# Latent projections in three mended products, retention's sums inside the next head, the last blocks turned one by one, and one head's value weights loaded aside

## What is computed

```python
# layer 1 of the first block, multi-head latent attention: h is normed and modulated, 768 x 1024
cq   = rms_norm(h @ w_dq, g_q)                  # 1024 -> 384
ckv  = h @ w_dkv                                # 1024 -> 256 + 64
c_kv = rms_norm(ckv[..., :256], g_kv); k_rope = rope(ckv[..., 256:])
# layer 2 of the first block, gated linear attention, 4 heads
q, k, v, gates = h @ w_q, h @ w_k, h @ w_v, log_sigmoid((h @ w1) @ w2 + b)
# layer 2 of the second block, retention, 4 heads of key width 256, value width 512
o = intra + inter                               # 512 tokens x 512 for each head
o = _standardize(o, 1e-6) * silu(gate)          # mean and variance over the 512 values
y = o @ w_out
# the end: layer_norm over 1024, result 512 x 1024
```

## Time and profile before

| | |
|---|---|
| median of 3 runs | 3577.15 us |
| profiled execution: its time, its span | 3580.42 us, 3578.7 us |
| PE busy | 3407.8 us (95%) |
| DVE, ACT, POOL busy | 1955.7, 1265.0, 229.4 us |
| chain that ended last: PE, DVE, ACT, issue, DMA | 86%, 7%, 2%, 2%, 2% |
| mean granted TensorE clock | 0.980 |

### The profile page before, as it was taken

How to read it: one execution, slowest core, us unless ns; L and a number is a source line. 1 busy time by engine, 2 the same in 40 slices (tenths; PEclk the granted TensorE clock), 3 DMA queues, 4 the chain that set the end, 5 groups by cost and what they waited for, 6 DMA issues and landing times.

```text
span 3578.7 us, 46166 instructions
## 1 busy us (share of the span) xinstructions
PE 3407.8 (95%) x17566; PEld 2887.0 (81%) x17566; DVE 1955.7 (55%) x2769; ACT 1265.0 (35%) x1635; POOL 229.4 (6%) x388
## 2 busy tenths in 40 slices
PE   8999989999998999999989999899998999999998
PEld 3799979999987887788868888678787777778886
DVE  4765564445446564645567677577635333454434
ACT  3354552312324333433353344332323222433332
POOL 1110011101000000111100000121100000000000
PEclk9999999999999999999999999999999999999999
DMA  6222123323320111454421111155533222222232
GB/s 231 82 72 65 59 76 111 109 92 118 98 78 30 53 48 59 162 164 156 152 80 36 35 35 48 48 188 188 165 93 101 71 70 70 69 74 94 93 95 80
DMA packets 295528, 335.36 MB, mean 94 GB/s; under 512 B 16497, under 2 KB 264177, under 8 KB 295281
## 3 DMA queue, kind: packets, MB, share of 16 engines
q1 hardware_dynamic: 262352, 232.93, 20.6%
q0 software_dynamic: 29440, 96.49, 8.6%
q10 hardware_dynamic: 3617, 4.26, 0.4%
HBM read 331.55 MB, written 2.10 MB: 93 GB/s over the span
## 4 chain that ended last, share of the span: by engine, by line
PE 86%; DVE 7%; ACT 2%; issue 2%; DMA 2%; DVEq 0%; ACTq 0%; SPq 0%; POOLq 0%; POOL 0%
PE acc L798 67%; PE sc L798 6%; PE sc L1451 2%; PE sc L945 1%; PE acc L1451 1%; PE acc L1644 1%; DVE d_col L2543 1%; PE acc L1060 1%; DMA wring<-in_mlp_w 1%; DVE w_lo L2478 1%; DMA wring<-in_ada_w 1%; PE acc L1423 1%; ACT arena L1847 0%; DVE xT L3042 0%; PE acc L1308 0%
## 5 line engine op out<-in xcount | busy, mean ns | idle before, releaser
L798 PE MATMUL acc<-x_lo,w_hi 128*128 128x512 f32 (+1 forms) x2192 | 826.4, 377 | 1.7 <-DVE xT L3007 1.1
L2478 DVE TENSOR_TENSOR w_lo<-wring,w_hi 128x1024 fp32r<-128x1024 f32 (+3 forms) x444 | 486.6, 1134 | 547.4 <-ACT w_hi L1789 546.5
L1789 ACT ACTIVATE w_hi<-wring 128x1024 fp32r<-128x1024 f32 (+3 forms) x446 | 418.0, 983 | 978.8 <-DMA wring<-in_mlp_w 480.9
L798 PEld LDWEIGHTS acc<-x_lo,w_hi 128*128 128x128 f32 x2192 | 415.2, 189 | 66.7 <-issue 3.1
L798 PE MATMUL acc<-hid_hi,w_hi 128*128 128x512 f32 (+1 forms) x1120 | 412.2, 368 | 5.9 <-DVE arena L2624 3.5
L798 PE MATMUL acc<-hid_hi,w_lo 128*128 128x512 f32 (+1 forms) x1120 | 408.5, 365 | 0.0
L798 PE MATMUL acc<-x_hi_holes,w_hi 128*128 128x512 f32 x768 | 307.9, 401 | 16.4 <-DVE x_lo L2594 13.9
L798 PE MATMUL acc<-x_hi_holes,w_lo 128*128 128x512 f32 x768 | 303.3, 395 | 0.0
L798 PE MATMUL acc<-hid_lo,w_hi 128*128 128x384 f32 (+1 forms) x768 | 270.9, 353 | 0.0
L798 PE MATMUL acc<-x_hi_seq,w_hi 128*128 128x512 f32 x576 | 228.5, 397 | 15.1 <-DVE x_lo L2597 12.6
L798 PEld LDWEIGHTS acc<-hid_hi,w_hi 128*128 128x128 f32 x1120 | 210.7, 188 | 32.9 <-DVE arena L2624 5.8
(11 more groups left out here) (463 smaller groups left out, 6210.5 us busy)
## 6 DMA issues: line engine op xcount, KB each, us to landing
wring<-in_mlp_w SPq DMA_DIRECT2D x64, 1024.0 KB, 5.5
rows_or_mod<-in_ada_w POOLq DMA_DIRECT2D x208, 256.0 KB, 3.2
wring<-in_ffn_up SPq DMA_DIRECT2D x44, 1024.0 KB, 5.1
wring<-in_ret_w_in SPq DMA_DIRECT2D x24, 1024.0 KB, 5.1
rstd<-in_ada_w POOLq DMA_DIRECT2D x88, 256.0 KB, 3.3
wring<-in_ffn_down SPq DMA_DIRECT2D x32, 704.0 KB, 4.7
wring<-in_gdn_w_in SPq DMA_DIRECT2D x16, 1024.0 KB, 6.0
tab<-in_ada_w POOLq DMA_DIRECT2D x40, 256.0 KB, 3.3
```

The source lines that it names most:

```text
L798: ins = pe.matmul(o, lhsT, rhs, start=start, stop=stop)
L1789: f(w_hi[s][:, c], (wring[s] if src is None else src)[:, c], ACT.Copy).then_inc(w_high, 1)
L2478: tt(w_lo[s][:, c], (wring[s] if src is None else src)[:, c], w_hi[s][:, c].bitcast(F32), SUB).then_inc(w_split, 1)
```

## The change

Four edits, independent of each other.

1. `mla_in` joins `SPLIT` with four weight groups (256 and 128 columns of w_dq, the 64 rotary columns, the 256 others of w_dkv). ACT makes `x_hi` of each block, DVE `x_lo` between two pieces; PE takes units 0 and 1 together, block by block, then units 2 to 5 (3 is now the rotary keys), with the sums of cq among them. ACT copies the units out instead of DVE. DVE's splits of the later groups stand at pieces 12, 21 and 28. The wait for the split rotary keys moves from before the heads to before the scores.
2. Retention's two sums leave the end of the head: `head_total` goes ahead of block 2 and `head_variance` ahead of block 5 of the next head's first unit (after the last head, of the output projection's first unit), with places in `sc`. The head has 10 units instead of 12. The first head is written out before the loops.
3. The last blocks: PE turns a block when it is ready, for all four token tiles, into 8 half tiles of 512 columns; DVE copies six of them, ACT two, and SP makes 8 stores.
4. The value weights of the first gated head are loaded to `v_side` once the key weights are split, and ACT copies their high parts before it copies the keys out.

```diff
-    ("mla_in", 1, 2, 6), ("mla_rope", 1, 0, 2), ("mla_pair", 4, 2, 32), ("mla_out", 1, 4, 8),
+    ("mla_in", 1, 4, 6), ("mla_rope", 1, 0, 2), ("mla_pair", 4, 2, 32), ("mla_out", 1, 4, 8),
...
-    ("ret_head", 4, 6, 12), ("ret_out", 1, 8, 8),
+    ("ret_head", 4, 6, 10), ("ret_out", 1, 8, 8),
...
+HALF_COLS["mla_in", 1], HALF_COLS["mla_in", 2] = DB * P // 2, DB * ROPE // 2
...
         g_out = carve(DB, SEQ)
+        v_side = arena[:, G_OUT_AT + DB * 256:G_OUT_AT + 2 * DB * 256]

...
+
+        def o_psum(h, t):
+            return acc[:, t, h, :] if t < 2 else sc[:, 3 - t, h, :]
+
+        def o_copy(h, t):
+            if h == 0:
+                return o_moved, t + 1
+            return (o_moved_late, t + 1) if t < 2 else (o_moved, LT + t - 1)
...
-            load("mla_in", 0, 0, blocks(A["mla_w_dq"][0]), DB, Q_RANK)
-            load("mla_in", 0, 1, blocks(A["mla_w_dkv"][0]), DB, KV_RANK + ROPE)
+            dq, dkv = blocks(A["mla_w_dq"][0]), blocks(A["mla_w_dkv"][0])
+            load("mla_in", 0, 0, dq[:, :, 0:2 * P], DB, 2 * P)
+            load("mla_in", 0, 1, dq[:, :, 2 * P:3 * P], DB, P)
+            load("mla_in", 0, 2, dkv[:, :, KV_RANK:KV_RANK + ROPE], DB, ROPE)
+            load("mla_in", 0, 3, dkv[:, :, 0:KV_RANK], DB, KV_RANK)
...
-                load("gla_head", it, 2, gv[:, :, bass.ds(it * GLA_DV, GLA_DV)], DB, GLA_DV)
+                if first:
+                    sp.wait_ge(w_split, half_group("gla_head", 0, 1, 1))
+                    sp.dma_start(v_side.rearrange("p (k n) -> p k n", k=DB), gv[:, :, 0:GLA_DV]).then_inc(w_loaded[GROUP0["gla_head"] % 2], 16)
+                else:
+                    load("gla_head", it, 2, gv[:, :, bass.ds(it * GLA_DV, GLA_DV)], DB, GLA_DV)
...
-            for t in range(LT):
-                sp.wait_ge(o_moved, t + 1)
-                sp.dma_start(out[0, t * P:(t + 1) * P, :], o_tok[:, t, :]).then_inc(out_done, 16)
-            sp.wait_ge(out_done, 16 * LT)
+            for h, t in o_order:
+                moved, n = o_copy(h, t)
+                sp.wait_ge(moved, n)
+                c = slice(h * 512, (h + 1) * 512)
+                sp.dma_start(out[0, t * P:(t + 1) * P, c], o_tok[:, t, c]).then_inc(out_done, 16)
+            sp.wait_ge(out_done, 16 * 2 * LT)
...
-            w = group("mla_in", 0, 0, DB, Q_RANK)
-            for j in range(6):
-                if j == 3:
-                    w = group("mla_in", 0, 1, DB, KV_RANK + ROPE)
-                claim(pe, "mla_in", 0, j)
-                linear(unit("mla_in", j), w, (j % 3) * P, all_h, T, DB,
-                       rows=P if j < 5 else ROPE, after=0 if j == 0 else None).then_inc(acc_ready, 1)
-                if j in (2, 3, 5):
-                    first_chunk({2: 0, 3: 1, 5: 2}[j])
...
+            S = "mla_in"
+            w = split_group(S, 0, 0, DB, 2 * P)
+            for k in range(DB):
+                pe.wait_ge(in_split, k + 1)
+                if k == DB // 2:
+                    second_half(S, 0, 0)
+                for j in range(2):
+                    last = split_product(unit(S, j), w, j * P, k, x_parts(T, k), k == 0, k == DB - 1)
+                    if k == DB - 1:
+                        last.then_inc(acc_ready, 1)
+
+            def latent(j, g, m, rows=P):
+                claim(pe, S, 0, j)
+                for k in range(DB):
+                    if m == 0 and k == DB // 2:
+                        second_half(S, 0, g)
+                    last = split_product(unit(S, j), w, m, k, x_parts(T, k), k == 0, k == DB - 1, rows)
+                last.then_inc(acc_ready, 1)
+
+            w = split_group(S, 0, 1, DB, P)
+            latent(2, 1, 0)
+            first_chunk(0)
+            w = split_group(S, 0, 2, DB, ROPE)
+            latent(3, 2, 0, ROPE)
+            square_sum("cq", T, range(2))
+            first_chunk(1)
+            w = split_group(S, 0, 3, DB, KV_RANK)
+            latent(4, 3, 0)
+            square_sum("cq", T, range(2, 3))
+            latent(5, 3, P)
+            first_chunk(2)
...
-            square_sum("cq", T)
             square_sum("ckv", T)
             first_chunk(3)
...
-            pe.wait_ge(krope_ready, 4)
...
+                pe.wait_ge(krope_ready, 4)
...
+            def head_total(it):
+
+                for j in range(2):
+                    emptied(pe, "ret_head", it, 8 + j, 1)
+                for b in range(4):
+                    last = pe.matmul(sc[:, 0, 0, :], ones, r_o[:, b, :], start=b == 0, stop=b == 3)
+                last.then_inc(r_total, 1)
+
+            def head_variance(it):
+
+                for b in range(4):
+                    pe.wait_ge(r_sq, it * 4 + b - 3)
+                    last = pe.matmul(sc[:, 0, 1, :], ones, r_sqr[:, b, :], start=b == 0, stop=b == 3)
+                last.then_inc(r_var, 1)
...
+                        if stage == "ret_out" and j == 0 and k == 2:
+                            head_total(RET_H)
+                        if stage == "ret_out" and j == 0 and k == 5:
+                            head_variance(RET_H)
...
-                        if first and b == 0:
+                        if first and not opening and b == 0:
+                            if k == 2:
+                                head_total(it)
+                            elif k == 5:
+                                head_variance(it)
+                        if first and opening and b == 0:
                             input_split(k, DB * 5)
...
+            for b in range(DB):
+                pe.wait_ge(x_ready, 56 + b + 1)
+                for t in range(LT):
+                    if t == LT - 1 and b in range(4, DB - 1):
+                        continue
+                    for k in range(4, DB) if t == LT - 1 and b == DB - 1 else (b,):
+                        last = turn_out(t, k)
+                    if b in (3, DB - 1):
+                        last.then_inc(o_turned, 1)
...
+                free(f(halves(dst), unit("mla_in", j)[0:rows, :, 0:HALF], ACT.Copy), "mla_in", j)
+
+            moved(0, cq[:, 0, :])
...
+            squares("cq", cq_at, T, None, range(2))
+            high_weights("mla_in", 0, 2)
+            moved(2, cq[:, 2, :])
+            high_weights("mla_in", 0, 3)
+            moved(3, kraw[0:64], ROPE)
+            emptied(act, "mla_in", 0, 2)
+            squares("cq", cq_at, T, None, range(2, 3))
+            moved(4, ckv[:, 0, :])
             act.wait_ge(uq_in, 48)
             high_weights("mla_pair", 0, 0)
             deviation("cq", T, Q_RANK)
-            squares("ckv", lambda b: ckv[:, b, :], T, lambda b: emptied(act, "mla_in", 0, 3 + b))
+            emptied(act, "mla_in", 0, 4)
+            squares("ckv", ckv_at, T, None, range(1))
+            moved(5, ckv[:, 1, :])
+            emptied(act, "mla_in", 0, 5)
...
+            high_lat(range(3))
...
+            deviation("ckv", T, KV_RANK)
             act.wait_ge(krope_ready, 2)
             for e in range(2):
                 f(krope_hi[e][:, :], krope[:, e, :], ACT.Copy).then_inc(krope_high, 1)
-            high_lat(range(3))
-            deviation("ckv", T, KV_RANK)
             high_lat(range(3, 5))
             scale = (NOPE + ROPE) ** -0.5
...
+                    high_weights(S, it, 2, src=v_side)
                     keys()
-                    high_weights(S, it, 2)
...
-            def ret_head(it, final):
+            def head_deviated(it):
+                for b in range(4):
+                    act.wait_ge(r_cent, it * 4 + b - 3)
+                    f(r_sqr[:, b, :], r_o[:, b, :], ACT.Square).then_inc(r_sq, 1)
+                act.wait_ge(r_var, it * 1)
+                f(rstd[:, 0:SEQ], sc[:, 0, 1, :], ACT.Ln, scale=1.0 / RET_DV, bias=eps[:, 0:1]).then_inc(r_logged, 1)
+                act.wait_ge(r_logged, it * 1)
+                f(rstd[:, 0:SEQ], rstd[:, 0:SEQ], ACT.Exp, scale=-0.5).then_inc(r_dev, 1)
+
...
+                        head_deviated(it)
                     finished(act, S, it, i)
...
+                act.wait_ge(o_turned, LT + t + 1)
+                f(o_tok[:, t, 512:1024], o_psum(1, t), ACT.Copy).then_inc(o_moved_late, 1)
...
+            split_weights("mla_in", 0, 0)
...
+            for b in range(DB):
+                dve.wait_ge(in_high, b + 1)
+                tt(x_lo[:, b, :], hT[:, b, :], x_hi[:, b, :].bitcast(F32), SUB).then_inc(in_split, 1)
+                if b < DB - 1:
+                    between(b)
+            split_weights("mla_in", 0, 1)
+            for p in range(DB - 1, FIRST_PIECES):
...
+                if p == 12:
+                    split_weights("mla_in", 0, 2)
+                elif p == 21:
+                    split_weights("mla_in", 0, 3)
+                elif p == 28:
+                    split_weights("mla_pair", 0, 0)
...
+            normed_latents("cq", range(3), "mla_g_q")
...
+            low_latents(range(3))
...
+            normed_latents("ckv", range(3, 5), "mla_g_kv")
+            for e in range(2):
+                dve.wait_ge(krope_high, e + 1)
```

(27 more changed lines are left out.)

217 lines of the change are left out of this document (92 added, 125 removed).

## The result

The kernel after takes 3542.48 us (median of 5 executions, 3540.57 to 3551.63); the kernel before took 3578.66 beside it (5 executions, 3573.24 to 3581.54). The ratio is 0.9916, 95% interval 0.9902 to 0.9930: 30 us less by the ratio, 36 by the medians. Two later series of the same pair gave 3546.35 beside 3574.25 (0.9924, 0.9910 to 0.9938) and 3546.66 beside 3578.88 (0.9914, 0.9901 to 0.9927). The profiled execution took 3540.57, with a span of 3538.9 and a mean granted clock of 0.984 against 0.980: 39.8 us of span less.

The account below looks back on a forecast made before the run. The prediction took PE, busy 95% of the span, as the bound. Gains of 14.5 + 8.0 + 3.6 + 6.1 = 32.2 us took the median from 3577.15 to 3545.0, range 3538 to 3556.

Parts of the forecast that it names:

- Part 1: Latent projections: cheaper split products bring the heads' first rotation 14.5 us earlier, bounds 16 and 8.
- the last group: Latent projections: last weight group, wanted at 99.8, has its first half split at 98; fits by 2 us.
- DVE's chain: Latent projections: DVE's work from the rope to the copy of the first queries takes 12.5 us.
- DVE sets the pace: Latent projections, units 0 and 1: DVE takes 2.35 us a block against PE's 2.1; units done at 76.6.
- DVE ends last: Latent projections' tail: DVE's work ends after PE's 132.9, so the heads' first rotation comes at 134.4.
- Part 2: Retention: moving the sums saves 2.8 us at each of three transitions, less 0.4; 8.0 in all, bounds 9 and 4.
- Part 3: Kernel end: turning the last blocks as they become ready gains 3.6 us, between 2.2 and 4.3.
- the bound by 262 GB/s: Kernel end: storing 2.1 MB at this rate takes 8.0 us from 3568.5, ending at 3576.5.
- Part 4: First gated head: removing the wait before the value units gains 6.1 us, bounds 3.3 and 6.4.
- the half clock which followed the gap: First gated head: nearly 6 us at half rate, 2.8 us lost, would go with the 3.35 us gap.
- Rival (b): Gated head and before output block 12: gaps go but half clocks stay or move; 2.8 + 1.5 less, 3549.3; chance 0.12.
- Rival (a): Latent projections give only half: DVE or a small load holds PE some 6 us, with half clock; 3552; chance 0.12.
- Rival (c): Latent projections: waits of 0.25 at each block keep PE at half clock most of the stage; 3587; chance 0.02.

Follow-up runs that it names:

- the wide ones: Kernel after with four output blocks moved before block 12 and gate products of all gated heads at 128 rows: 0.9881; with the pairs' eight sums at 128 rows too: 0.9897.
- the parts alone: Four kernels, each the kernel before with one edit: latents 0.9981, retention 0.9975, end 0.9999, gated head 0.9991.
- the whole: The kernel after with all four edits, unchanged, run again in two later series: ratios 0.9924 and 0.9914.
- the kernel without latents: The kernel after without the latent projections' edit, keeping retention, end and gated head: 3558.04 beside 3578.88, ratio 0.9936.

## Why the prediction was right

The forecast was 3545.0 in 3538 to 3556, faster with 0.94; the kernel takes 3542.5 to 3546.7 in three series. The sum was 32.2; the three series give 30, 27 and 31 by their ratios. Step by step, with each term as the step of the table less what the same place shows in kernels without the part:

- **Part 1, 14.5 forecast.** The price of a product (0.174), the last group with nothing to spare and DVE's chain of 12.05 (forecast 12.5) behind the rope held. The step "DVE sets the pace" did not, though its number did (units 0 and 1 end near 76.4, forecast 76.6): PE never waits for a block behind the first, and what holds it back is the half clock of the first 3.4 us (a cost of 1.5), which it doesn't catch up. The size was too large. Nine traces with this part (those of later kernels too) have 11.5 to 15.5, mean 13.2; less 1.3 it is 11.9. The mis-sized term is mainly the half clock: the prediction let it fall on the first block alone and hid the rest under DVE's chain. In five of the nine the stretch at the start is 6.8 and not 3.4 (0.5 to 1.3 us more). Four have one near 101, 3.4 us long (a cost of 1.7), which nothing hides; in all four PE waits 0.2 to 2.1 us before unit 4 for the split of the last group, and the four traces without this wait have no such stretch, nor has the one where it is 0.1. Sums of one column and squares lie ahead of the wait, so it isn't shown which of them brings the clock down. Five have one from 120 to 125, 3.4 or 6.8 long. It uses up the 1.3 us that PE would wait for DVE's copy: L1053 waits 1.3 in the four traces without it and 0.1 to 0.2 in these five, so "DVE ends last" held in four of nine. The first trace had one stretch in the whole stage, and alone would have made the term look exact. The four passes of the Trainium skill (FP8 and Floating Point Precision, TensorE Precision Notes) would have given 7.9 a unit; 8.43 and 8.32 stand here, so the row of before was the better price.
- **Part 2, 8.0 forecast.** 8.7 as the mean of seven traces. Each transition gave 3.3 in the first trace (a head's period is 87.45 instead of 90.74), not 2.8: a record outlasts the distance to the next (in the kernel after the eight records of a sum last 3.60, and the next product starts 3.03 behind their start; the last product of the outputs lasts 0.25 beyond the next start), and a wait exposes this tail, which the idle time in the brackets leaves out. Two waits, two tails: 2.81 + 0.57 + 0.25 = 3.6, an estimate and 0.3 over what was measured. The fourth gave nothing, as forecast, and in some executions costs a half clock too (8.3 and 8.5 in the table).
- **Part 3, 3.6 forecast.** 3.0 to 3.9 in the table, mean 3.6, and 4.5 against what kernels without it show there. The issue of eight stores took 4.51, so the last came 4.0 behind the last normed block, not 3.1, and the bound by 262 GB/s did not bind: from 3531 to 3538 the kernel after moved 299 GB/s.
- **Part 4, 6.1 forecast.** 5.0 as the mean of six traces, 3.2 less what others show. This step failed: "the half clock which followed the gap" was booked on the gap. It began within the gap (at 1117.9, 2.2 behind the last thin product and 1.2 before the gap's end). The gap of 3.35 was all but taken away and the clock fell still, since the eight products of 16 rows ahead of it bring it down. The two kernels with doubled and shortened gate products, and the wide ones, show it.

The net terms are 11.9 + 8.7 + 4.5 + 3.2 = 28.3, inside the three series. Too much in parts 1 and 4 (5.5) stood against too little in parts 2 and 3 (1.6); that the forecast of the time came out within 3 us of the first median is partly luck, as that series had the largest difference of medians (36.2, against 27.9 and 32.2). Rival (b) came true in half: the half clock stayed in the gated head and comes and goes before block 12. Rival (a) did not come in the first trace, where DVE's list ended at 118.1 and the last group was in time, and came in small in others: the wait before unit 4 is 0.1 to 2.1 us in five of nine traces, with a half clock in four of them, and not the 6 us of the rival. Rival (c) did not come either, and not by its own argument: PE had no waits at the blocks behind the first, and the clock was back at 1.00 at 61.3. So the oscillation that the Trainium skill describes (TensorE: Matmul & The Clock Gate, HAM oscillation) isn't seen at the blocks, for want of waits there. The time of this rival, 3587, is 3545 + 42; the 3555 + 32 of the prediction gives the same number by other terms.

What stays open: why the three other parts together bring 23 us and alone 12. The errors nearly cover it (10 us, against 9 from the four intervals), and the parts alone ran on another chip than the whole and the kernel without latents, each beside the kernel before on its own. The mean clock takes away most of it: freed of the clock (mean of span times granted clock over the executions) the kernel before has 3506.7, the parts alone 3494.9, 3496.0, 3505.2 and 3505.7, that is 11.8 + 10.7 + 1.5 + 1.0 = 25.0, and the whole 3479.7 and 3479.0 beside 3505.9 and 3507.8, that is 26.2 and 28.8. The kernel without latents has 3491.5 beside 3507.8, 16.3, where its three parts alone have 13.2, with a standard error of 2 on the first. So what exceeds the sum lies mainly in the granted clock, and why that was higher isn't shown. At the end, where PE waits, this way of counting is rough.

## What to carry to other kernels

Put a price on the clock apart from the wait: ask what PE does in the microseconds ahead of a place where the clock falls, and whether it falls before the gap is over. If these are products of few rows, test them as the cause before the gap: fill them up to 128 rows with zeros where space allows. That cost no time on PE here. When a number comes out as forecast, look whether its wait is there: units 0 and 1 ended on time without the wait that was to time them. Compare the same record in several traces, with a stage that was not touched beside it, before a gain of a few microseconds is put down to an edit; one trace of before and one of after carry 5 us of chance.

## What the runs showed of the hardware

- Eight products of 16 rows (2.5 us) in the first gated head were followed by 3.4 us at 0.50 in six of six traces with PE idle for 0.23 us at most; sixteen by 6.8 us without any idle, in one. In the later gated heads this came in 21 of 36 cases, and at the eight sums over 8 and 16 rows (3.7 us at full clock) in 41 of 52, 3.4 or 6.8 us long; the longer ones began before the sums were over. The same products with 128 rows, of which the rest are zeros, took the same time (0.32 and 0.43 from one to the next), and no such stretch came at the gated heads in two traces and at the pairs in one.
- Other stretches have another cause, or none that was found: the wait of 2.7 us before output block 12 had one in four of seven traces, waits of 0.2 to 2.1 us before unit 4 of the latents, behind sums of one column, in four of four, a wait of 0.1 none.
- The kernel before spreads over 20 us (3562 to 3584 in 35 executions) at mean clocks of 0.979 to 0.985; the stretch from 1130 to 2760 us alone differs by 15.7 us between traces of kernels that have the same code there.
